# Attention steps regrouped over two key heads, and the last chunk of the residual handled in halves

## The reference, cut to what matters

```python
q = partial_rope((hn @ w_q).reshape(1, 512, 16, 64))        # 16 query heads of 64
# 4 key heads; query head h uses key head h // 4; window 128, blocks of 128 queries
s = einsum('bnqkgd,bnjkd->bnkgqj', qb, kk) * 64 ** -0.5      # keys: this block and the one before
m = maximum(max(s), sink)                                   # one sink per query head
w = exp(s - m) / (sum(exp(s - m)) + exp(sink - m))
o = einsum('bnkgqj,bnjkd->bnqkgd', w, vv)
h = h + o @ w_o
h = h + square(relu(rmsnorm(h) @ w_up)) @ w_down
gate = sigmoid(rmsnorm(h) @ w_ple_gate)
h = h + gate * (p @ w_ple_proj)
return rmsnorm(h, norm_final)
```

## Time and profile before

| what | us |
|---|---|
| median of three runs | 1762.11 (1760.16 to 1765.09) |
| the profiled execution, whole time | 1762.08 |
| its span, first to last instruction | 1760.3 |
| TensorE busy in it | 1730.7 (98%) |
| GpSimd, VectorE, ScalarE busy | 982.0, 887.8, 771.6 |
| mean granted TensorE clock | 0.994 |

### The profile page before, as it was taken

The page is one execution under the profiler, slowest core; times in us unless marked ns, Lnnn a source line. Parts: engine busy times, 40 slices in busy tenths (PEclk is TensorE's granted clock), DMA queues, the critical chain, the costliest instruction groups (busy, mean ns, idle before and its releaser), DMA issues.

```text
span 1760.3 us, 20968 instructions
## 1 busy us (share of the span) xinstructions
PE 1730.7 (98%) x8018; PEld 1414.7 (80%) x8018; DVE 887.8 (50%) x1293; ACT 771.6 (44%) x1208; POOL 982.0 (56%) x614
## 2 busy tenths in 40 slices
PE   9999999999999999999999999999999999999998
PEld 7888888777788888888888888886667888888886
DVE  3999997667774966512121212746564221212124
ACT  5323335377867754343232323523664432323234
POOL 5859655667678456644444446655446444444464
PEclk9999999999999999999999999999999999999999
DMA  4222323222253243222222222231012222222221
GB/s 170 97 96 91 113 96 121 93 75 84 96 203 135 82 129 126 96 96 96 96 96 96 99 99 99 86 97 66 31 37 84 94 98 96 96 96 96 96 96 60
DMA packets 55540, 172.05 MB, mean 98 GB/s; under 512 B 6416, under 2 KB 14224, under 8 KB 54544
## 3 DMA queue, kind: packets, MB, share of 16 engines
q1 hardware_dynamic: 55440, 170.70, 28.6%
HBM read 164.65 MB, written 6.03 MB: 97 GB/s over the span
## 4 chain that ended last, share of the span: by engine, by line
PE 68%; DVE 6%; ACT 3%; issue 2%; POOL 2%; DMA 1%; SPq 0%; POOLq 0%; DVEq 0%; ACTq 0%
PE B L313 55%; PE B L2263 2%; PE B L2171 2%; PE B L2372 1%; PE B L2376 1%; PE B L2374 1%; PE B L2245 1%; DVE SW L1142 1%; PE B L296 1%; DVE B L1012 1%; PE B L298 0%; PE B L297 0%; PE B L2110 0%; PE B L1872 0%; PE B L1410 0%
## 5 line engine op out<-in xcount | busy, mean ns | idle before, releaser
L289 POOL TENSOR_TENSOR WL<-RAW,WH 128x1024 fp32r<-128x1024 f32 x281 | 681.2, 2426 | 609.9 <-ACT WH L285 609.8
L285 ACT ACTIVATE WH<-RAW 128x1024 fp32r<-128x1024 f32 x281 | 297.0, 1059 | 635.5 <-PE B L313 601.1
L313 PE MATMUL B<-P0h,WH 128*128 128x512 f32 x1104 | 432.8, 392 | 3.2 <-DVE Yl L426 1.8
L313 PE MATMUL B<-P0l,WH 128*128 128x512 f32 x1104 | 425.1, 390 | 1.4 <-DVE P0l L430 1.3
L313 PE MATMUL B<-P0h,WL 128*128 128x512 f32 x1104 | 278.4, 389 | 0.0
L313 PEld LDWEIGHTS B<-P0h,WH 128*128 128x128 f32 x1104 | 207.3, 188 | 48.9 <-DVE Yl L426 2.7
L313 PEld LDWEIGHTS B<-P0l,WH 128*128 128x128 f32 x1104 | 207.3, 188 | 45.5 <-DVE P0l L430 2.3
L313 PEld LDWEIGHTS B<-P0h,WL 128*128 128x128 f32 x1104 | 207.2, 188 | 43.1
L437 DVE TENSOR_TENSOR H<-H,B 128x512 f32<-128x512 f32 x88 | 60.2, 686 | 288.0 <-PE B L313 288.0
L313 PE MATMUL B<-P1h,WH 128*128 128x512 f32 x448 | 174.7, 390 | 0.0
L1941 DVE SCALAR_TENSOR_TENSOR TMP<-B,RS 128x512 f32<-128x512 f32 x64 | 44.1, 691 | 258.4 <-PE B L313 244.0
(11 more groups left out here) (351 smaller groups left out, 2752.8 us busy)
## 6 DMA issues: line engine op xcount, KB each, us to landing
RAW<-in_w SPq DMA_DIRECT2D x281, 512.0 KB, 3.2
PX<-in_zeros SPq DMA_DIRECT2D x4, 1024.0 KB, 9.5
H<-in_xT SPq DMA_DIRECT2D x8, 256.0 KB, 5.1
g<-GB SPq DMA_DIRECT2D x8, 256.0 KB, 2.2
GB<-g SPq DMA_DIRECT2D x32, 64.0 KB, 2.0
out<-Q SPq DMA_DIRECT2D x4, 512.0 KB, 3.6
CA<-in_zeros SPq DMA_DIRECT2D x1, 1920.0 KB, 10.4
u<-TMP SPq DMA_DIRECT2D x7, 256.0 KB, 2.0
```

The costliest lines, as they stand in the source:

```text
L285: act.activation(WH[:, i % NS, :], RAW[:, i % NR, :], ACT.Copy).then_inc(*inc("w_hi", i))
L289: pool.tensor_tensor(WL[:, i % NS, :], RAW[:, i % NR, :], WH[:, i % NS, :].bitcast(F32), ALU.subtract).then_inc(*inc("w_lo", i))
L313: return pe.matmul(b[:, :], w[:, ws[c]], x[:, c, :], start=start, stop=stop)
```

## The change

Step n now is a pair of key heads a = n // 8, a pair of chunks hp = n // 4 % 2 and block n % 4: two query heads of each of the two key heads. Scores alternate between partitions 0 to 63 and 64 to 127, each half into a bank of its own. The products with the values alternate between output partitions 0 to 63 and 64 to 127 of one bank, with 256 positions each, so that the result is 128 partitions x 256. The sinks are reordered to match. For the end, chunk 7's gate, square and scaling run in two halves of 256 positions through `tmp(2)`, and the sums, the mean and the root are taken for blocks 0 and 1 and for blocks 2 and 3 by themselves. The diff's core:

```diff
@@ act_last_ple, act_last_halves, dve_last_halves
+            if n == 7:
+                act_last_halves(act)
+                continue
+    def half(t):
+        return slice(256 * t, 256 * t + 256)
+    def act_last_halves(act):
+        b = tmp(2)
+        for t in range(2):
+            act.wait_ge(*at("evac_d", ("last", t)))
+            act.activation(b[:, half(t)], b[:, half(t)], ACT.Sigmoid).then_inc(*inc("ple_sig", ("last", t)))
+        for t in range(2):
+            if t:
+                act.wait_ge(*at("h", ("ple", 1, 7)))
+            else:
+                act.wait_ge(*at("h", ("last", 0)))
+                act.wait_ge(*at("acc", ("out", 5)))
+            act.activation(tmp(1)[:, half(t)], H[:, 7, half(t)], ACT.Square).then_inc(*inc("sq", ("last", t)))
+            act.activation(PJ[:, 7, half(t)], H[:, 7, half(t)], ACT.Copy, scale=vec("norm_final", 7)).then_inc(
+                *inc("weighted", (7, t)))
+    def dve_last_halves(dve):
+        b, x, what = tmp(2), ple_bank(1, 7), ("gate1", 0, 7)
+        dve.wait_ge(*at("unit", what))
+        dve.wait_ge(*at("rs", ("spread", "ple1")))
+        for t in range(2):
+            dve.tensor_tensor(b[:, half(t)], x[:, half(t)], rs("ple1")[:, half(t)], ALU.mult).then_inc(*inc("evac_d", ("last", t)))
+        dve.wait_ge(*at("evac_a", ("pj", 1, 7)))
+        dve.wait_ge(*at("h", ("down1", 3, 7)))
+        for t in range(2):
+            dve.wait_ge(*at("ple_sig", ("last", t)))
+            dve.tensor_tensor(b[:, half(t)], b[:, half(t)], PJ[:, 7, half(t)], ALU.mult).then_inc(*inc("ple_y", ("last", t)))
+            dve.wait_ge(*at("ple_y", ("last", t)))
+            dve.tensor_tensor(H[:, 7, half(t)], H[:, 7, half(t)], b[:, half(t)], ALU.add).then_inc(
+                *(inc("h", ("ple", 1, 7)) if t else inc("h", ("last", 0))))
@@ place, pe_scores
-        kv, blk = n // 4, n % 4
-        return kv, blk, (128 if blk == 0 else 0), (128 if blk == 0 else 256), slice(64 * (kv % 2), 64 * (kv % 2) + 64)
+        a, hp, blk = n // 8, n // 4 % 2, n % 4
+        return a, 4 * a + 2 * hp, blk, (128 if blk == 0 else 0), (128 if blk == 0 else 256)
+    HALF = [slice(0, 64), slice(64, 128)]
-        for hp in range(2):
-            b, before = banks.take(("s", n, hp), "att_s")
+        bs = []
+        for hf in range(2):
+            b, before = banks.take(("s", n, hf), "att_s")
             pe.wait_ge(*at(*before))
-            pe.wait_ge(*at("rope", ("q", 4 * (kv // 2) + 2 * hp + 1)))
-            for j in range(2):
-                c = 4 * (kv // 2) + 2 * hp + j
-                last = pe.matmul(b[:, 256 * j:256 * j + nk], Q[p_, c, 128 * blk:128 * blk + 128], KT[p_, kv // 2, ks],
-                                 start=True, stop=True)
-            last.then_inc(*inc("unit", ("s", n, hp)))
+            bs.append(b)
+        pe.wait_ge(*at("rope", ("q", c0 + 1)))
+        for j in range(2):
+            for hf, p_ in enumerate(HALF):
+                last = pe.matmul(bs[hf][:, 256 * j:256 * j + nk], Q[p_, c0 + j, 128 * blk:128 * blk + 128],
+                                 KT[p_, a, ks], start=True, stop=True)
+                if j:
+                    last.then_inc(*inc("unit", ("s", n, hf)))
@@ pe_out, out_parts
-        for i, hf in enumerate(halves(n)):
-            pe.wait_ge(*at("evac_a", ("wt", n, hf)))
-            last = pe.matmul(b[p_, :], V[:, blk - 1 + hf, 64 * kv:64 * kv + 64], wt_buf(n, hf), start=i == 0,
-                             stop=i == len(halves(n)) - 1)
+        for i, kh in enumerate(halves(n)):
+            pe.wait_ge(*at("evac_a", ("wt", n, kh)))
+            for hf, p_ in enumerate(HALF):
+                kv = 2 * a + hf
+                last = pe.matmul(b[p_, 0:256], V[:, blk - 1 + kh, 64 * kv:64 * kv + 64],
+                                 wt_buf(n, kh)[:, 256 * hf:256 * hf + 256], start=i == 0, stop=i == len(halves(n)) - 1)
-        cs, ts = slice(4 * (kv // 2), 4 * (kv // 2) + 4), slice(128 * blk, 128 * blk + 128)
-        return P1h[p_, cs, ts], P1l[p_, cs, ts], banks.bank["o", n][p_, :].rearrange("p (c t) -> p c t", c=4)
+        cs, ts = slice(c0, c0 + 2), slice(128 * blk, 128 * blk + 128)
+        return P1h[:, cs, ts], P1l[:, cs, ts], banks.bank["o", n][:, 0:256].rearrange("p (c t) -> p c t", c=2)
@@ pe_turn, pe_end, act_end, dve_end, pool_end
-        pe.wait_ge(*at("weighted", c))
+        pe.wait_ge(*(at("weighted", (7, j // 2)) if c == 7 else at("weighted", c)))
...
-        sums(ACC[:, :], first=True)
-        for j in range(3):
+        for t in range(2):
+            sums(ACC[:, :], t)
+        for j in range(2):
             for c in range(7):
                 pe_turn(pe, c, j)
-        pe.wait_ge(*at("sq", ("out", 7)))
-        sums(tmp(1), last=True).then_inc(*inc("stat_sums", "out"))
+        pe.wait_ge(*at("sq", ("last", 0)))
+        sums(tmp(1), 0, last=True).then_inc(*inc("stat_sums", ("last", 0)))
+        for c in range(7):
+            pe_turn(pe, c, 2)
+        pe.wait_ge(*at("sq", ("last", 1)))
+        sums(tmp(1), 1, last=True).then_inc(*inc("stat_sums", ("last", 1)))
         for j in range(3):
             pe_turn(pe, 7, j)
...
-        act.wait_ge(*at("stat_root", "out"))
         for j in range(4):
+            act.wait_ge(*at("stat_root", ("last", j // 2)))
...
-        stat_mean(dve, "out")
-        dve.wait_ge(*at("stat_root", "out"))
+        for t in range(2):
+            b = banks.bank["sums", ("out", t)]
+            dve.wait_ge(*at("stat_sums", ("last", t)))
+            dve.tensor_scalar(SM[:, 4 + 2 * t:6 + 2 * t], b[:, 0:2], 1e-6, None, ALU.add).then_inc(
+                *inc("stat_ms", ("sums", ("out", t))))
         for j in range(4):
+            dve.wait_ge(*at("stat_root", ("last", j // 2)))
...
-        stat_root(pool, "out")
+        for t in range(2):
+            pool.wait_ge(*at("stat_ms", ("sums", ("out", t))))
+            pool.tensor_tensor(SM[:, 8 + 2 * t:10 + 2 * t], SM[:, 4 + 2 * t:6 + 2 * t], SM[:, 0:2], ALU.pow).then_inc(
+                *inc("stat_root", ("last", t)))
```

More of the change, by code:

```diff
@@ L2067, in dve_last_ple @@
         for c in range(8):
+            if c == 7:
+                dve_last_halves(dve)
+                continue
             if c != 1:
@@ L2158, in place @@
     def place(n):
-        kv, blk = n // 4, n % 4
-        return kv, blk, (128 if blk == 0 else 0), (128 if blk == 0 else 256), slice(64 * (kv % 2), 64 * (kv % 2) + 64)
+        a, hp, blk = n // 8, n // 4 % 2, n % 4
+        return a, 4 * a + 2 * hp, blk, (128 if blk == 0 else 0), (128 if blk == 0 else 256)
+    HALF = [slice(0, 64), slice(64, 128)]
     def pe_scores(pe, n):
-        kv, blk, k0, nk, p_ = place(n)
+        a, c0, blk, k0, nk = place(n)
         ks = slice(128 * blk - 128 + k0, 128 * blk + 128)
-        for hp in range(2):
-            b, before = banks.take(("s", n, hp), "att_s")
+        bs = []
+        for hf in range(2):
+            b, before = banks.take(("s", n, hf), "att_s")
             pe.wait_ge(*at(*before))
-            pe.wait_ge(*at("rope", ("q", 4 * (kv // 2) + 2 * hp + 1)))
-            for j in range(2):
-                c = 4 * (kv // 2) + 2 * hp + j
-                last = pe.matmul(b[:, 256 * j:256 * j + nk], Q[p_, c, 128 * blk:128 * blk + 128], KT[p_, kv // 2, ks],
-                                 start=True, stop=True)
-            last.then_inc(*inc("unit", ("s", n, hp)))
+            bs.append(b)
[6 more added lines that the diff above has]
+                    last.then_inc(*inc("unit", ("s", n, hf)))
     def s_buf(n, hp):
@@ L2178, in s_view @@
     def s_view(n, hp):
-        nk = place(n)[3]
+        nk = place(n)[4]
         return s_buf(n, hp).rearrange("p (a k) -> p a k", a=2)[:, :, 0:nk]
@@ L2195, in dve_maxima @@
     def dve_maxima(dve, n):
-        kv = place(n)[0]
         st = AS[:, n, :]
@@ L2201, in dve_maxima @@
                 *inc("att_d", (n, "max", hp)))
-        sk = sink[:, 4 * kv:4 * kv + 4]
+        sk = sink[:, 4 * (n // 4):4 * (n // 4) + 4]
         dve.wait_ge(*at("att_d", (n, "max", 1)))
@@ L2501, in pe_end, with sums @@
         assert len(banks.queue) == 8
[L2502 to L2508, removed]
+        for t in range(2):
+            _, before = banks.take(("sums", ("out", t)), "stat_ms")
+            pe.wait_ge(*at(*before))
+        def sums(x, t, last=False):
+            b = banks.bank["sums", ("out", t)]
+            for j in range(2):
+                p = pe.matmul(b[:, j:j + 1], x[:, 256 * t + j * 128:256 * t + j * 128 + 128], MEAN[:, 0:1],
+                              start=not last and j == 0, stop=last and j == 1)
             return p
         pe.wait_ge(*at("acc", ("out", 6)))
-        sums(ACC[:, :], first=True)
-        for j in range(3):
+        for t in range(2):
+            sums(ACC[:, :], t)
+        for j in range(2):
             for c in range(7):
                 pe_turn(pe, c, j)
-        pe.wait_ge(*at("sq", ("out", 7)))
-        sums(tmp(1), last=True).then_inc(*inc("stat_sums", "out"))
```

(5 more changed lines are left out.)

## The result

The changed kernel takes 1748.45 us in the median (1746.99 to 1749.03, four runs), the kernel before 1762.7 in the same session (1760.16 to 1765.09). The ratio is 0.9921 with a 95% interval of 0.9909 to 0.9933. By the ratio the change saves 13.9 us; the two medians are 14.25 apart.

What follows compares the result with a forecast made beforehand. TensorE was taken to bound the kernel: 14.2 us saved in attention less 1.3 and 2.5 lost keeps 10.4, plus 1.3 at the end makes 11.7, so 1762.1 - 11.7 = 1750.4 us; own range 1745 to 1755.

Steps and rivals of the forecast that it cites:

- What bounds the kernel: Attention and the MLP behind: TensorE sets the pace, busy 122.43 of 125 us, so its savings reach the end.
- Scores and out: TensorE in attention: overlapping halves save 6.0 us in scores, 7.4 plus 0.8 in out; 14.2, bounds 0 and 22.4.
- five slots: Scores and out in attention: records keep their order, so eight take five slots of 0.216 us, ideally saving 0.65 in scores.
- What eats into it: Attention: VectorE and ScalarE hold TensorE back, losing 1.3 us at the first wait and 2.5 in iterations 8 to 11.
- the wait before scores(4): First TensorE wait in attention, 1.57 us: 0.7 us of savings lost, 0.6 more as scores wait for both banks.
- The loop between VectorE and ScalarE: Attention: its own period falls from about 6.4 to about 6.0 us, against a TensorE iteration of 6.5.
- The clock: Attention, after the first wait: 3.5 us at half clock left as is; bounds -1.7 and +3.4 us.
- The end: Last chunk in halves: the first store comes 1.3 us earlier, bounds 0.3 to 2.0.
- the slower one: Rival: switching halves in scores and out empties the array and nothing overlaps; +9 us, 1771; chance 0.10.
- serial records: Rival: scores and out records follow each other at 0.216 us, only the end gains; 1760.8; chance 0.13.
- column halves: Rival: row halves overlap but column halves don't, so out saves 0 and scores 6.0; 1756.6; chance 0.12.
- The rival in which the losses are 8.5: Attention: overlap as forecast, but loop and half-clock windows take 8.5 us in place of 3.8; 1755.1; chance 0.12.

Runs made afterwards that it cites:

- experiment 2: The changed kernel with scores and out products ordered lower, lower, upper, upper instead of alternating; 1748.04 us, ratio 0.9925 to the kernel before.
- e5: The changed kernel with GpSimd's low parts in attention waiting for VectorE's small operations of the maxima; 1744.04 us, ratio 0.9899 to the kernel before.
- e1_attention_only: The kernel before with only the regrouped scores and outs, its end left as before; 1749.36 us, ratio 0.9931.
- e3_grouped: The changed kernel with products listed lower, lower, upper, upper instead of alternating; 1748.04 us, ratio 0.9925 to the kernel before.
- e4_short_maxima: The changed kernel with maxima over 2 keys and scores scaled down, not the reference's softmax; 1737.18 us, ratio 0.9864 to the kernel before.

## Why the prediction was right

1748.45 against 1750.4 forecast, in its own range of 1745 to 1755. The mechanism was right: two halves overlap, and the loop takes a part back. Its two sizes were both wrong, by 9.6 us too little saved and 6.3 too little lost. Attention kept 13.7 where I had forecast 10.4, and in the profiled execution the 2.0 us lost elsewhere brought the total closer. That the total came within 2 us is luck.

- *What bounds the kernel.* Right. The MLP behind attention kept its pace (TensorE 100.00 of 100 us in 1400 to 1500), so what attention kept reached the end.
- *Scores and out, 14.2 us, bounds 0 and 22.4.* Direction right, term too small: 23.8, over my upper bound. Three errors. I let the records leave in order, five slots; experiment 2 shows that the order is of no account here, and the times are those of four slots. I took 0.11 us for a weight load as a limit for both halves together; in the block 0 steps the 8 loads of the scores took 0.52 us where they took 0.96 before, so loads of two halves run beside each other. And I held the scores of those steps to be at that limit and worth nothing, and their outs worth 0.2, where they gave 0.44 and 0.42 each, 3.4 in all in place of 0.8. The scores of the block 0 steps are what took the sum over the bound.
- *What eats into it, 3.8 us.* Too small: 10.1. Two places were right: the wait before scores(4) and the iterations 8 to 11. A third was missing: 2.2 us of waits before out(13) and out(14), at 1303.60 and 1309.37, behind an L2253 that was held for 2.40 us at 1298.04; e5 has 0.2 there. The sizes were wrong. The loop between VectorE and ScalarE, about 6.0 us, was sized well: in e5, without the long hold, VectorE goes from scores(10) to scores(11) in 5.87.

```profile
1271.91 1.28 DVE L2241 SCALAR_TENSOR_TENSOR TMP<-B,CO 128x512 f32<-128x512 f32 x2
...
1277.78 1.28 DVE L2241 SCALAR_TENSOR_TENSOR TMP<-B,CO 128x512 f32<-128x512 f32 x2
```

But I compared it with a TensorE iteration of 6.5, which at four slots is 5.92 (1285.30 to 1291.22). So almost no margin was left even in the iterations of twelve fillers, and a long hold was passed on. I named the holds and gave them no price of their own; taking the longest out gave 4.2. The wait before scores(4) became 4.0 us, not 1.6 plus a share. Counted from scores(0), the bank that scores(4) waits for was free 1.0 us earlier than before (its records start after 23.80 us in place of 24.81), as I had forecast. But TensorE was there 2.7 us earlier, by its larger saving.
- *The clock.* One half-clock stretch more in attention, behind the 2.7 us wait: within the bounds given. Their pattern isn't explained: `e1_attention_only` and `e3_grouped`, with the same two waits, have one stretch of about 7 us behind the first and none behind the second.
- *The end, 1.3 us.* Right: 1.44 in the trace. The root over two columns took 0.71 instead of 1.02, which I had not counted.
- *The rivals.* No cost of switching halves (the slower one), no serial records, and column halves overlap as row halves do: four out records of 512 columns took 1.86 us, and eight of 256 take 1.01, with their eight loads in 0.63 us beside running products (PEld of L2313 at 1286.37). The Trainium skill's rule, in "TensorE: Matmul & The Clock Gate", Part 3, that a load overlaps matmuls only when its row group differs, does not hold for them here. What the same section of the Trainium skill says of matmuls in distinct groups, that they run together, does hold. The gain is better than by its ratios, about 0.78 of the ideal: 1.92 / 1.07 = 1.79 is 0.90 of it. The rival in which the losses are 8.5 was nearest on that term; with the overlap sized in full it gives 1762.1 - (23.8 - 8.5) - 1.3 = 1745.5.
- *What would show it.* The signs pointed the right way, but two values lie outside them: scores took 1.07 us where I gave 1.1 to 1.5, and an iteration 5.92 where I gave about 6.5.

## What to carry to other kernels

When an engine that is 98% busy gets faster in one stage, set its new pace beside the round trip of the other engines through their waits, not beside their busy time: at 62% busy VectorE's loop of 5.9 us was as long as TensorE's new iteration. Then look for small operations that are held or queued behind something unrelated: two edits that were worth 4.8 us of the stage while TensorE covered a part of the delays were worth 9.1 afterwards. And if products have only 64 rows or 64 columns, give both halves of the array work: here they came in pairs for the price of one.

## What the runs showed of the hardware

- Float32 products in different row halves of the array start within one 20 ns window and run side by side: eight records of 256 columns in 1.07 us instead of 1.92. Column halves do as well: eight records in 1.01 us, where four of twice the columns took 1.86. Both hold, within 0.02 us, when the program lists two products of one half before two of the other (`e3_grouped`).
- Weight loads of two row halves don't queue behind one another: eight with 128 columns in 0.52 us instead of 0.96 (PEld of L2218 at 1255.20, of L2171 at 1258.45 before).
- A VectorE operation on 128 x 4 numbers can take 1.57 us when a GpSimd subtraction of 2.38 us runs, and ends 0.02 us after it.
- TensorE's granted clock was at its lower level (0.51) for about 3.4 us behind waits of 4.0 and 2.7 us, and at 0.57 over the 4 us from 341, in code that was not changed. A longer wait was not always followed by a lower clock: the 1.57 us wait of the kernel before was, and one of 2.0 us in `e4_short_maxima` was not.
